# First loads of a fused attention and convolution layer in two halves of the contraction, input rows ahead of the modulation weights

## The reference

```python
ada = silu(c) @ w_ada + b_ada                  # 1 x 3072
shift, scale, gate = split(ada, 3)
h = x * (1 + scale) + shift                    # 2048 x 1024
proj = h @ w_in + b_in                         # 2048 x 8704, ten parts
```

## Time and profile before

| | us |
|---|---|
| median of three runs | 2014.13 (2011.61 to 2014.8) |
| profiled execution, its time | 2009.24 |
| its span | 2007.5 |
| TensorE busy in it | 1920.3 (96%) |
| first product of group 0 starts at | 58.35 |
| product 6 of group 0 starts at | 82.66 |

### The profile page before, as it was taken

One profiled execution on the slowest core, in us unless ns is written; L12 is line 12 of the kernel. 1 busy time (PEld: TensorE's weight loads), 2 busy tenths in 40 slices (PEclk: granted clock), 3 DMA queues, 4 the chain that ended last, 5 costly groups with the idle time before them and its releaser, 6 DMA issues. The chain is left out here.

```text
span 2007.5 us, 25472 instructions
## 1 busy us (share of the span) xinstructions
PE 1920.3 (96%) x8989; PEld 1517.8 (76%) x8989; DVE 1228.4 (61%) x2168; ACT 857.6 (43%) x1512; POOL 201.1 (10%) x356
## 2 busy tenths in 40 slices
PE   3799999999999999999998999999999999999996
PEld 3588888777777777777776777778887878887885
DVE  5655564445666666655666666667657565556775
ACT  2544453444455445466676544444344510012221
POOL 0022211111000000011211000000011100000000
PEclk9899999999999999999998999999999999999998
DMA  8566743343222232255764232223245688883441
GB/s 311 194 194 188 231 163 113 111 110 90 79 76 78 79 90 82 73 167 161 256 218 164 72 95 79 81 74 76 85 153 158 206 218 226 239 288 123 142 144 74
DMA packets 303645, 289.03 MB, mean 144 GB/s; under 512 B 38340, under 2 KB 255552, under 8 KB 299808
## 3 DMA queue, kind: packets, MB, share of 16 engines
q1 hardware_dynamic: 277280, 199.01, 34.3%
q0 software_dynamic: 26240, 88.40, 12.3%
HBM read 198.97 MB, written 88.38 MB: 143 GB/s over the span
## 5 line engine op out<-in xcount | busy, mean ns | idle before, releaser
L1018 PE MATMUL acc<-t_hi,w_hi 128*128 128x512 f32 x1904 | 771.9, 405 | 19.2 <-ACT room L1195 8.0
L1020 PE MATMUL acc<-t_lo,w_hi 128*128 128x512 f32 x1904 | 747.2, 392 | 0.0
L1021 PE MATMUL acc<-t_hi,w_lo 128*128 128x512 f32 x1904 | 745.6, 392 | 0.0
L1018 PEld LDWEIGHTS acc<-t_hi,w_hi 128*128 128x128 f32 x1904 | 358.8, 188 | 131.3 <-issue 49.7
L1021 PEld LDWEIGHTS acc<-t_hi,w_lo 128*128 128x128 f32 x1904 | 359.0, 189 | 79.3
L1020 PEld LDWEIGHTS acc<-t_lo,w_hi 128*128 128x128 f32 x1904 | 359.4, 189 | 68.2 <-issue 0.2
L1430 DVE TENSOR_TENSOR room<-acc,part 128x512 f32<-128x512 f32 x204 | 140.8, 690 | 224.8 <-PE acc L1021 223.1
L1234 ACT ACTIVATE part<-acc,cols 128x512 f32<-128x512 f32 x204 | 140.2, 687 | 244.3 <-PE acc L1021 244.0
L1430 DVE TENSOR_TENSOR room<-room 128x512 f32<-128x512 f32 (+3 forms) x222 | 178.3, 807 | 92.3 <-DMA room<-wg_d 41.8
L1216 ACT CAST w_hi<-w_raw 128x512 fp32r<-128x512 f32 x272 | 167.6, 616 | 97.8 <-PE acc L1021 95.7
L1430 DVE TENSOR_TENSOR w_lo<-w_raw,w_hi 128x512 fp32r<-128x512 f32 x272 | 184.2, 685 | 29.6 <-ACT w_hi L1216 29.5
(11 more groups left out here) (204 smaller groups left out, 2072.7 us busy)
## 6 DMA issues: line engine op xcount, KB each, us to landing
w_raw<-in_w_in SPq DMA_DIRECT2D x136, 512.0 KB, 5.2
gate_d<-room POOLq DMA_DIRECT2D x64, 256.0 KB, 2.7
w_raw<-gate_d SPq DMA_DIRECT2D x32, 512.0 KB, 5.2
qk_d<-room POOLq DMA_DIRECT2D x24, 512.0 KB, 4.3
room<-qk_d SPq DMA_DIRECT2D x192, 64.0 KB, 2.7
ada_w<-in_w_ada SPq DMA_DIRECT2D x8, 1024.0 KB, 11.9
room<-in_x SPq DMA_DIRECT2D x32, 256.0 KB, 6.1
t_raw<-tr_d SPq DMA_DIRECT2D x8, 1024.0 KB, 8.2
```

The costliest lines, as they stand in the source:

```text
L1018: nc.tensor.matmul(to, w_hi[:, s, k], t_hi[:, p, k], start=(first and k == 0), stop=False, skip_group_check=True)
L1020: nc.tensor.matmul(to, w_hi[:, s, k], t_lo[:, p, k], start=False, stop=False, skip_group_check=True)
L1021: mm = nc.tensor.matmul(to, w_lo[:, s, k], t_hi[:, p, k], start=False, stop=(last and k == KH - 1), skip_group_check=True)
```

## The change

The sum for shift and scale moves from DVE to TensorE: a matmul per slice k and per part (shift, scale), with the column `c_act[:, k]` as the stationary operand and 512 columns of weights as the moving one, float32, into one row of PSUM; ACT and DVE copy the row to SBUF, eight transposes of one partition each make columns of it. The weights come in two halves (columns 0 to 511 and 512 to 1023 of shift and of scale, `kh` 0 and 1), each in eight DMAs of 512 KB. The loads of x go first. Products 0 and 1, which need only `kh` 0, come before the second half's sum is done. Operand 4 is formed earlier on DVE, operand 6 one step earlier, and a dump to DRAM changes place. Some semaphores late in the kernel are shared (`t_in` for `wp_in` and `wo_in`), with the same waits.

```diff
+                def load_ada(half):
+                    for q in range(KT // 2):
+                        for k in (2 * q, 2 * q + 1):
+                            src = w_ada2[k, :, 0:2 * D].rearrange("p (s n) -> p s n", s=2)[:, :, half * CH:(half + 1) * CH]
+                            sp.dma_start(ada_w[half][:, k], src).then_inc(ada_in[half * KH + q], 16)
                 for i in range(4):
                     load_x(i)
+                load_ada(0)
                 load_w(0)
-                for i in range(4, 16):
+                for i in range(4, 8):
+                    load_x(i)
+                load_ada(1)
+                for i in range(8, 16):
                     load_x(i)
                 load_w(1)
...
@@ GpSimd
+                pool.wait_ge(h_ready, 16)
+                pool.dma_start(tr_d[0, 3], hs[:, 3]).then_inc(dumped["b21"], 16)
                 pool.wait_ge(t1_ready, 2)
                 pool.dma_start(tr_d[0, 2], hs[:, 0]).then_inc(dumped["rest"], 16)
-                pool.wait_ge(h_ready, 16)
-                pool.dma_start(tr_d[0, 3], hs[:, 3]).then_inc(dumped["b21"], 16)
...
@@ TensorE
+                def turn_x(u):
+                    pe.wait_ge(h_ready, 4 * u) if u else pe.wait_ge(cols_done, 1)
+                    for i in range(4 * u, 4 * u + 4):
+                        pe.wait_ge(x_in[i % 6], 16 * (i // 6 + 1))
...
+                def turn_last_x():
+                    pe.wait_ge(mod_ready, 4)
+                    for i in range(12, 16):
+                        pe.wait_ge(x_in[i % 6], 16 * (i // 6 + 1))
+                    for kk in range(KH):
+                        if kk >= 2:
+                            pe.wait_ge(h_ready, 8 + kk - 1)
...
+                def ada_product(half, q):
+                    pe.wait_ge(ada_in[half * KH + q], 32)
+                    for k in (2 * q, 2 * q + 1):
+                        for j in range(2):
+                            mm = nc.tensor.matmul(acc[0:1, (0, 1)[j] if half == 0 else (1, 3)[j]], c_act[:, k:k + 1],
+                                                  ada_w[half][:, k, j], start=(k == 0), stop=(k == KT - 1))
+                    if q == KT // 2 - 1:
+                        mm.then_inc(row_done, 1)
+
+                def ada_columns(half):
+                    pe.wait_ge(row_copied, 2 * half + 2)
+                    for n in range(2 * KH):
+                        tr = nc.tensor.transpose(acc[:, 2 if half == 0 else 1, n:n + 1],
+                                                 ada_row[0:1, half, n // KH, n % KH * P:(n % KH + 1) * P], ident[0:1, 0:1])
+                    tr.then_inc(ada_done, 1)
+
+                turn_x(0)
+                pe.wait_ge(c_ready, 1)
+                for q in range(KT // 2):
+                    ada_product(0, q)
+                ada_columns(0)
+                turn_x(1)
...
-                        if g == 0:
-                            pe.wait_ge(h_ready, 16)
...
+                product(0)
+                turn_x(2)
+                for q in range(3):
+                    ada_product(1, q)
+                product(1)
+                ada_product(1, 3)
+                ada_columns(1)
+                turn_last_x()
                 for n in range(NS):
-                    product(n)
+                    if n >= 2:
+                        product(n)
...
@@ ACT
+                copy_row(0)
                 modulate(0)
                 first_t(0)
-                modulate(1)
                 for n in range(2):
                     round_w(n)
+                modulate(1)
                 first_t(1)
-                modulate(2)
                 for n in range(2, 4):
                     round_w(n)
+                copy_row(1)
+                modulate(2)
+                modulate(3)
                 first_t(2)
-                modulate(3)
...
@@ DVE (the sum over ada_w is gone)
+                def modulation(half):
+                    dve.wait_ge(row_done, half + 1)
+                    nc.vector.tensor_copy(ada_row[0:1, half, 1], acc[0:1, (1, 3)[half]]).then_inc(row_copied, 1)
                     dve.wait_ge(ada_done, half + 1)
...
+                modulation(0)
                 for n in range(3):
                     combine(0, n)
                 first_t_lo(0)
+                split_w(0)
+                split_w(1)
                 dve.wait_ge(h_ready, 8)
                 tt_op(t1_raw[:], hs[:, 1], hs[:, 0], ALU.subtract).then_inc(t1_ready, 1)
-                split_w(0)
-                split_w(1)
                 dve.wait_ge(t1_ready, 1)
                 first_t_lo(1)
+                split_w(2)
+                modulation(1)
                 dve.wait_ge(h_ready, 12)
                 dve.wait_ge(dumped["b11"], 16)
                 tt_op(hs[:, 0], hs[:, 2], t1_raw[:], ALU.subtract).then_inc(t1_ready, 1)
-                split_w(2)
+                tt_op(hs[:, 1], hs[:, 2], hs[:, 1], ALU.subtract).then_inc(t1_ready, 1)
                 first_t_lo(2)
...
                     if m < 4:
-                        if m == 1:
-                            dve.wait_ge(t1_ready, 1)
-                            tt_op(hs[:, 1], hs[:, 2], hs[:, 1], ALU.subtract).then_inc(t1_ready, 1)
-                        if m == 3:
+                        if m == 2:
                             dve.wait_ge(dumped["b21"], 16)
                             dve.wait_ge(t1_ready, 2)
                             dve.wait_ge(h_ready, 16)
```

More of the change, by code:

```diff
@@ L416, in build @@
         ya_done = sem("ya_done")
-        wp_in = [sem(f"wp_in{r}") for r in range(4)]
         wp_hi_done = sem("wp_hi_done")
@@ L966, in _ @@
                 nc.tensor.transpose(xb[:, 0:NCOL], vecs, ident[0:NCOL, 0:NCOL]).then_inc(cols_turned, 1)
[L967 to L983, removed]
-                    for kk in range(KH):
-                        tr = nc.tensor.transpose(turn_banks[u % 2][kk][:, (i % 4) * P:(i % 4 + 1) * P],
-                                                 xt[:, i % 6, kk * P:(kk + 1) * P], ident[:])
-                    tr.then_inc(x_turned, 1)
+                def turn_x(u):
[3 more added lines that the diff above has]
+                        for kk in range(KH):
+                            tr = nc.tensor.transpose((sc_ps[:, 0], sc_ps[:, 1], po[:], xb[:])[kk][:, (i % 4) * P:(i % 4 + 1) * P],
+                                                     xt[:, i % 6, kk * P:(kk + 1) * P], ident[:])
+                        tr.then_inc(x_turned, 1)
@@ new lines, in turn_last_x @@
+                def turn_last_x():
+                    pe.wait_ge(mod_ready, 4)
+                    for i in range(12, 16):
+                        pe.wait_ge(x_in[i % 6], 16 * (i // 6 + 1))
+                    for kk in range(KH):
+                        if kk >= 2:
+                            pe.wait_ge(h_ready, 8 + kk - 1)
+                        for i in range(4):
+                            tr = nc.tensor.transpose((acc[:, 1], acc[:, 3], sc_ps[:, 0], sc_ps[:, 1])[kk][:, i * P:(i + 1) * P],
+                                                     xt[:, (12 + i) % 6, kk * P:(kk + 1) * P], ident[:])
+                        tr.then_inc(x_turned, 1)
@@ L1438, in _ @@
                 own_t.wait()
-                own_t.up(tt_op(c_act[:], c_e[:], cols[:, C_C:C_C + KT], ALU.mult))
-                own_t.wait()
-                for k in range(KT):
-                    dve.wait_ge(ada_in[k], 16)
-                    if k == 0:
-                        own_t.up(nc.vector.tensor_scalar(acc_a[:], ada_w[:, k], c_act[:, k:k + 1], None, ALU.mult))
-                    elif k < KT - 1:
-                        own_t.up(nc.vector.scalar_tensor_tensor(out=acc_a[:], in0=ada_w[:, k], scalar=c_act[:, k:k + 1],
-                                                                in1=acc_a[:], op0=ALU.mult, op1=ALU.add))
-                    else:
-                        for half in range(2):
-                            a, w = (v.rearrange("p (s n) -> p s n", s=2)[:, :, half * CH:(half + 1) * CH]
-                                    for v in (acc_a[:], ada_w[:, k]))
-                            nc.vector.scalar_tensor_tensor(out=a, in0=w, scalar=c_act[:, k:k + 1], in1=a,
-                                                           op0=ALU.mult, op1=ALU.add).then_inc(acc_done, 1)
-                    if k < KT - 1:
-                        own_t.wait()
@@ L1456, in _ @@
-                for half in range(2):
+                tt_op(c_act[:], c_e[:], cols[:, C_C:C_C + KT], ALU.mult).then_inc(c_ready, 1)
+                def modulation(half):
+                    dve.wait_ge(row_done, half + 1)
+                    nc.vector.tensor_copy(ada_row[0:1, half, 1], acc[0:1, (1, 3)[half]]).then_inc(row_copied, 1)
                     dve.wait_ge(ada_done, half + 1)
                     o = slice(half * KH, (half + 1) * KH)
-                    q = slice(KT + o.start, KT + o.stop)
+                    from_ps = acc[:, (2, 1)[half]]
@@ L1460, in _ @@
                     b = slice(C_ADA + o.start, C_ADA + o.stop)
```

(6 more changed lines are left out.)

35 lines of the change are left out of this document (22 added, 13 removed).

## The result

The changed kernel takes 2020.77 us, the median of 8 runs (2017.47 to 2023.57), against 2011.39 of the kernel before in 8 runs (2006.77 to 2015.53). The ratio is 1.0042, 95% interval 1.0029 to 1.0055: **slower by 8.5 us, between 5.8 and 11.1**, which is 0.4%. The forecast was 4.8 us slower. The sign was right, the size too small.

What follows compares the result with a forecast made beforehand. TensorE, busy 96%, was taken as the bound, with product 6's start deciding: 60.6 + 26.9 = 87.5 against 82.66, 4.8 later, so 2014.1 + 4.8 = 2018.9 us. Range 2008 to 2027; the forecast's own +1.5 to +9.

Steps and rivals of the forecast that it cites:

- the mark: Start of product 6 on TensorE, after which it always has work; forecast at 87.5 against 82.66, 4.8 later.
- The price of a plain matmul: Sum on TensorE: a 512-column float32 matmul costs 0.86 in a stream at the high clock, 1.7 at the low.
- Rival B: Sum on TensorE: a plain matmul costs 1.04 to 1.12, about +11, 2025; chance 0.08.
- rival C: Sum on TensorE: matmuls run faster than 0.86, deciding below 0.56; -1.5 to -5.6, down to 2009; chance 0.10.
- Rival A: Clock stays low in TensorE's sums: first half takes 27.3, product 6 at 111, +28.5, 2042.6; chance 0.15.
- The first loads: Start of the kernel: x 0 to 3 turned by 8.3, first quarter of new weights landed at 10.1, last 18.3.
- M: Moment when the second half's shift and scale are ready; forecast at 60.6.
- From M to the mark: Stretch from second shift and scale to product 6, through ACT's take and unbroken DVE passes; forecast 26.9.
- Rival D: Clock high all along once TensorE has work from 5 us on: +0.7, 2014.8, no difference; chance 0.10.

Runs made afterwards that it cites:

- the repeat: The changed kernel run once more, unaltered; ratio to the kernel before 1.0056 (1.0042 to 1.0071).
- second sum cut: The changed kernel without the twelve matmuls of the second half's sum that stand ahead of product 1; ratio to the kernel before 1.0017.
- unit 2 behind the sum: The changed kernel with product 1 behind unit 3's turning and unit 2 of x turned behind the second half's sum; ratio to the kernel before 1.0039.
- the halves on DVE: The changed kernel with its loads kept, each half summed on DVE and product 1 behind the last turns of x; ratio to the kernel before 0.9962.
- weight 3 in the gap: The halves on DVE, with combine(0, 3) and split_w(3) moved into DVE's wait for the third modulation; 2002.91 us, ratio to the kernel before 0.9956.

## Why the prediction was right or wrong

**The bound and the mark: right.** The mark moved by 7.0 while product 0 moved 20.7 the other way, and the time went with the mark. In the twelve rows of the table the time against before follows the mark's shift with a remainder of -1.7 to +5.0.

**The forecast of the time itself: closer than its working, by luck.** The forecast of 2018.9 stands on 2014.1 for the kernel before, which measured 2011.39 over eight runs. The two errors, 2.7 too high there and 3.7 too small in the step, leave 1.9. The step of 8.5 lies just inside the range of +1.5 to +9; that of the repeat (1.0056, +11.3, between 8.4 and 14.3) lies above it.

**The price of a plain matmul: right.** Forecast 0.86; measured 10.46 for 24 records, which are twelve matmuls, 0.87 each, with one stationary column as with the 128 of the earlier trace rows. Rival B (1.04 to 1.12) and rival C (under 0.56) fall with that row. Forecast 15.3 for the first half from a low clock; measured 15.41.

**Rival A, a low clock in the sums: wrong.** At the low clock 32 records would have taken 27. The weights of the first records were loaded at 12.81, 13.65, 14.50 and 15.36, from 16.07 on every 0.43: the pace doubled 3 us into the sum. In "second sum cut" the same sum took 16.70 and in "unit 2 behind the sum" 16.77, so when it rises differs by up to 1.5 us between executions.

**The first loads: the term that was mis-sized.** I let the first tiles of x run at 385 GB/s and the first quarter of the weights land at 10.1. It landed at 12.84; in the other executions that load x first it was first used at 12.0 to 13.2. Between 4 and 10 the windows add up to 2 x (256 + 209 + 320) = 1570 KB where 385 would have been 2310: 740 KB short, 1.9 us. The rows I took the rate from the earlier trace rows lie at 25 us, with other transfers under way. The queue was not empty in the slow stretch either. SP's timeline has the slices issued right behind the tiles:

```profile
2.29 1.78 SPq L559 DMA_DIRECT2D room<-in_x  x4
4.11 6.88 SPq L566 DMA_DIRECT2D ada_w_a<-in_w_ada  x8
```

Nor are the first transfers of a kernel always slow: in the same three windows the kernel before, with its slices of 1 MB first, moves 373, 401 and 434 GB/s, and the one with the 512 KB pieces first 331, 325 and 350. With the 256 KB tiles of x in front it is 209 to 320, and 182 to 370 in four other executions. Why is not shown.

The Trainium skill, in "DMA: Bandwidth & Descriptors", section Bandwidth, gives 341 GB/s for 1 MB transfers and less for small ones. The trace is under this figure for the first tiles (209 to 320) and above it for the queued pieces of 512 KB, 380 to 398.

The loads stayed late by as much: unit 2, which waited for x 8, was turned at 44.2 (forecast 41.5), and the second sum, which stands behind it, began 2.7 late. That is nearly all of the miss at M: 62.8 for 60.6. The sum and product 1 took 0.4 more than forecast; the copy, the turns and the scale took 1.7 where I had counted 2.6, which gave some back.

**From M to the mark: right.** Forecast 26.9, measured 26.8, and again 26.8 in every kernel of the table with the change's order behind M, but one (27.1, where x came late). Product 2 came at M + 10.3 (forecast 10.5), released by ACT's take.

**Rival D, the clock high all along: half right.** Product 0 ran at 0.23 per matmul from its start, 1.3 behind the last work; product 2, behind 8.15 of idling, began at 0.43 for nine matmuls. What product 0 saved by it went into the wait for x 8 behind it (0.99 at 41.70).

**Beyond the mark: not foreseen.** I forecast nothing there. The mark gives +7.0, the measured +8.5 holds it in its interval, but the repeat and the other versions with TensorE's sum show 1.8 to 5 us more. Its place in the trace is shown in part (1.6 between 340 and 600), its cause is open.

**The idea and its execution.** The forecast treated the halves, the earlier x and the engine as one change. The experiments take the engine apart from the rest: with the sum on DVE the change gains 7.3 of mark, and with it on TensorE, product 1 in its middle, it loses 7.0. They don't take the halves apart from the new order of the operands. The prediction put 7.3 down to that order, and the rows agree: the third modulation is no earlier than before (51.41 for 51.29), and the whole gain lies behind it. In the kernel before, DVE did the sum beneath its loads (1.3 per slice here, hidden); moving it to the engine whose work comes next put it on the path.

## What to carry to other kernels

Before a sum moves to TensorE, ask what hides it now and what stands behind it there: plain float32 cost 0.87 per 512 columns however few stationary columns it had, and what was added to the second half was wholly on the path. Split a change into its loads, its order and its engine before judging it: here the engine was wrong, the new order of the operands gave the gain, and the halves by themselves are not shown to give any. Take a transfer rate from rows with the same transfers at the same place: the 256 KB tiles ran at 209 to 320 GB/s at the start, where other first loads ran at 325 to 434.

## What the runs showed of the hardware

**The clock after a short idle stretch.** The same program started product 6 after the same wait (2.85 and 2.89) in two profiled executions. In the first it ran six matmuls at the high clock and then seven at the low one (granted clock 0.50 from 92 to 94), in the second all at the high one (1.00). TensorE's timeline of the first:

```profile
90.85 0.47 PE L1054 MATMUL acc<-t_hi,w_lo 128*128 128x512 f32 x1
91.12 0.63 PE L1051 MATMUL acc<-t_hi,w_hi 128*128 128x512 f32 x1
91.55 0.63 PE L1053 MATMUL acc<-t_lo,w_hi 128*128 128x512 f32 x1
...
94.49 0.40 PE L1054 MATMUL acc<-t_hi,w_lo 128*128 128x512 f32 x1
```

TensorE's timeline of the second, at the same place:

```profile
88.95 0.47 PE L1051 MATMUL acc<-t_hi,w_hi 128*128 128x512 f32 x1 [2.89 <-DVE room L1480]
...
90.86 0.39 PE L1054 MATMUL acc<-t_hi,w_lo 128*128 128x512 f32 x1
91.08 0.39 PE L1051 MATMUL acc<-t_hi,w_hi 128*128 128x512 f32 x1
91.31 0.39 PE L1053 MATMUL acc<-t_lo,w_hi 128*128 128x512 f32 x1
```

So the clock can fall when the idle stretch is over and the engine is at work again, and the seven matmuls at 0.43 cost 1.4 us in one execution and nothing in another.

**Transposes alone can bring the high clock.** With the sum on DVE, TensorE had been idle from 27 to 30.09 and then only turned x; the pace went from 0.21 to 0.11 among the sixteen transposes. TensorE's timeline of the halves on DVE:

```profile
30.57 0.42 PE L982 MATMUL pt_o<-ident,room 128*128 128x128 f32 x1
30.79 0.42 PE L982 MATMUL xb<-ident,room 128*128 128x128 f32 x1
...
33.07 0.27 PE L982 MATMUL pt_o<-ident,room 128*128 128x128 f32 x1
33.18 0.27 PE L982 MATMUL xb<-ident,room 128*128 128x128 f32 x1
```

It doesn't always come among them: in "weight 3 in the gap", the same program up to there, all sixteen ran at 0.21 (29.67 to 32.92), and product 0 began at the low clock 1.3 later. The rule of the Trainium skill that the prediction weighed ("TensorE: Matmul & The Clock Gate", Part 4, that transposes don't bring it) does not hold in the trace of the halves on DVE.
